# Modulation weights of a two-block network as fp32 products or as rounded halves and rests

## The reference, cut to what matters

```python
mod_x = (silu(c) @ w_mod + b_mod)[:, None, :]      # c: 1 x 1024, w_mod: 1024 x 6144
mod_c = silu(c_ctx) @ w_mod + b_mod
sh1, sc1, gt1, sh2, sc2, gt2 = split(mod_x, 6)     # and the same six of mod_c
h_x = rms_norm(x, g_norm1) * (1.0 + sc1) + sh1     # 256 x 1024
h_c = rms_norm(ctx, g_norm1) * (1.0 + csc1) + csh1
# h_x, h_c @ w_in: keys, values, gates ... ; later  x = x + gt1 * y_x,  and gt2, sc2, sh2
```

## Time and profile before

| | |
|---|---|
| median of 3 runs | 3134.74 us (3132.2 to 3134.81) |
| the profiled execution's own time | 3132.64 us |
| its span (first to last instruction) | 3130.8 us |
| mean granted TensorE clock | 0.956 |
| busy: PE, PEld, DVE, ACT, POOL | 92%, 76%, 63%, 49%, 6% |
| HBM read | 609.49 MB, 195 GB/s over the span |

### The profile page before, as it was taken

How to read it: one execution, slowest core, us unless ns; L and a number is a source line. 1 busy time by engine, 2 the same in 40 slices (tenths; PEclk the granted TensorE clock), 3 DMA queues, 4 the chain that set the end, 5 groups by cost and what they waited for, 6 DMA issues and landing times.

```text
span 3130.8 us, 42461 instructions
## 1 busy us (share of the span) xinstructions
PE 2866.4 (92%) x15757; PEld 2364.4 (76%) x15757; DVE 1960.3 (63%) x2198; ACT 1548.7 (49%) x1544; POOL 181.7 (6%) x204
## 2 busy tenths in 40 slices
PE   7999996999999998979999999999999999998997
PEld 1476785667666676758888897789788988977996
DVE  1345665888888888885568436554545674365554
ACT  2144444776777777663445444433334444354342
POOL 0000000000000000000036000000000440000000
PEclk9999997999999999998999999999989989999999
DMA  8522534898888989973243005544533430054454
GB/s 299 188 81 81 188 135 191 333 366 345 338 350 336 353 332 360 349 298 139 108 162 135 1 1 201 195 149 165 192 122 135 143 126 1 10 225 163 175 186 171
DMA packets 58072, 612.62 MB, mean 196 GB/s; under 512 B 12649, under 2 KB 18337, under 8 KB 21570
## 3 DMA queue, kind: packets, MB, share of 16 engines
q1 hardware_dynamic: 57922, 610.56, 51.6%
HBM read 609.49 MB, written 1.05 MB: 195 GB/s over the span
## 4 chain that ended last, share of the span: by engine, by line
issue 47%; PE 27%; DVE 10%; DMA 7%; POOL 5%; ACT 4%; DVEq 0%; SPq 0%; POOLq 0%; ACTq 0%
DVE arena_rounded L1514 7%; DMA weight_slabs<-in_expert_slabs 6%; ACT arena_rounded L1511 3%; PE psum_vector L562 3%; PE psum_vector L1567 2%; PE psum_vector L515 2%; PE psum_vector L517 2%; PE psum_vector L516 2%; POOL arena L3110 2%; PE psum_scalar L515 2%; PE psum_scalar L516 2%; PE psum_scalar L517 2%; PE psum_vector L1524 2%; PE psum_scalar L1554 2%; POOL arena L3113 2%
## 5 line engine op out<-in xcount | busy, mean ns | idle before, releaser
L1931 DVE TENSOR_TENSOR weight_slabs_rounded<-weight_slabs,arena_rounded 128x2048 fp32r<-128x2048 f32 x208 | 479.1, 2310 | 420.7 <-ACT arena_rounded L1928 403.4
L1514 DVE TENSOR_TENSOR arena_rounded<-weight_slabs,arena_rounded 128x2048 fp32r<-128x2048 f32 x290 | 651.9, 2287 | 62.9 <-ACT arena_rounded L1511 53.5
L1928 ACT ACTIVATE arena_rounded<-weight_slabs 128x2048 fp32r<-128x2048 f32 x208 | 396.2, 1913 | 455.6 <-PE psum_vector L517 261.4
L1511 ACT ACTIVATE arena_rounded<-weight_slabs 128x2048 fp32r<-128x2048 f32 x290 | 548.0, 1912 | 125.8 <-DMA weight_slabs<-in_expert_slabs 62.8
L515 PE MATMUL psum_vector<-arena_rounded,arena_rounded 128*128 128x512 f32 (+3 forms) x1312 | 480.1, 366 | 43.4 <-DVE weight_slabs_rounded L1931 30.8
L515 PE MATMUL psum_scalar<-arena_rounded,arena_rounded 128*128 128x256 f32 (+1 forms) x1456 | 476.2, 327 | 36.1 <-DVE weight_slabs_rounded L1931 15.5
L1554 PE MATMUL psum_scalar<-arena_rounded,arena_rounded 128*128 128x512 f32 x768 | 325.3, 424 | 71.8 <-DVE arena_rounded L1514 66.6
L517 PE MATMUL psum_vector<-arena_rounded,arena_rounded 128*128 128x512 f32 (+3 forms) x960 | 376.3, 392 | 0.0
L516 PE MATMUL psum_vector<-weight_slabs_rounded,arena_rounded 128*128 128x512 f32 x880 | 348.2, 396 | 0.0
L515 PEld LDWEIGHTS psum_scalar<-arena_rounded,arena_rounded 128*128 128x128 f32 x1456 | 283.4, 195 | 68.3 <-issue 13.5
L515 PEld LDWEIGHTS psum_vector<-arena_rounded,arena_rounded 128*128 128x128 f32 (+1 forms) x1312 | 257.6, 196 | 86.0 <-DVE weight_slabs_rounded L1931 41.2
(11 more groups left out here) (453 smaller groups left out, 4222.2 us busy)
## 6 DMA issues: line engine op xcount, KB each, us to landing
weight_slabs<-in_expert_slabs SPq DMA_DIRECT2D x145, 2048.0 KB, 9.1
weight_slabs<-in_layer_slabs SPq DMA_DIRECT2D x103, 2048.0 KB, 7.8
weight_slabs<-in_mixer_slabs SPq DMA_DIRECT2D x32, 2048.0 KB, 7.4
weight_slabs<-in_layer_slabs SPq DMA_DIRECT2D x6, 1024.0 KB, 5.4
arena<-in_mem SPq DMA_DIRECT2D x3, 1024.0 KB, 10.3
arena<-in_b_gate SPq DMA_DIRECT2D x6, 512.0 KB, 4.5
constants<-in_constants SPq DMA_DIRECT2D x1, 1025.0 KB, 5.0
arena<-in_x SPq DMA_DIRECT2D x1, 1024.0 KB, 7.2
```

Source lines behind the costliest of these rows:

```text
L1511: e.activation(high_, whole, ACT.Copy).then_inc(S("expert_high"), 1)
L1514: e.tensor_tensor(low, whole, high_.bitcast(F32), ALU.subtract).then_inc(S("expert_split"), 1)
L1928: e.activation(fr(high), low, ACT.Copy).then_inc(S("weights_high"), 1)
L1931: e.tensor_tensor(fr(low), low, fr(high).bitcast(F32), ALU.subtract).then_inc(S("weights_split"), 1)
```

## The change

Four rows take the place of two. ACT rounds silu(c) and silu(c_ctx) to a head each, DVE makes the rests; `c_parts` holds head and rest of c, head and rest of c_ctx. For slabs 1, 2, 4, 5, 6, 8, 9 and 10 the weights too are split, and a slab is 8 products with the head and 8 with the rest of the weights, all in rounded numbers, four stationary columns each. Slabs 0, 3, 7 and 11 stay fp32 products, of `c_whole` (the two vectors and two rows of zeros). The pairs of rows are added where rows become columns: the 16 transposes turn into 16 fp32 products of the 4-row result with a 4x2 table of ones and zeros; the gate rows add two rows in the same way. The heads of the mod slabs take turns at 64, 72, 88 and 96 KB. DVE and ACT split slab n + 1 before they turn to row n. The small loads move from behind slab 4 to behind slab 8, and ACT's order behind the evacuations changes with them.

```diff
-        for n in range(MOD_SLABS, len(MIX_SLABS)):
+        MIX_WHOLE = (0, 3, 7, 11)
+        MIX_SPLIT = [n for n in range(len(MIX_SLABS)) if n not in MIX_WHOLE]
+        MIX_RINGS = {1: (64, 72, 88, 96), 12: (88, 96, 104), 16: (112, 120, 128), 18: (120, 128), 20: (88, 128, 48), 26: (88, 120, 104)}
+        for n in MIX_SPLIT:
...
+        def mod_ahead(n):
+            return 2 * len([k for k in MIX_SPLIT if k <= min(n + 1, MOD_SLABS - 1)]) - 1
...
-                if n == 4:
+                if n == 8:
                     sp.wait_ge(S("set_by_pool"), 1)
...
+            def mod_rows(n):
                 w = slab()
                 bank = V.open()
+                if n in MIX_WHOLE:
+                    for k in range(KC):
+                        mm = pe.matmul(bank[0:4, :], c_whole[:, :, k], w[:, k, :], start=k == 0, stop=k == KC - 1)
+                    V.close(mm)
+                else:
+                    for i in range(2):
+                        high, low = half()
+                        for k in range(4):
+                            pe.matmul(bank[0:4, :], c_parts[:, :, 4 * i + k], high[:, k], start=i + k == 0, stop=False)
+                            mm = pe.matmul(bank[0:4, :], c_parts[:, :, 4 * i + k], low[:, k], start=False, stop=i == 1 and k == 3)
+                        if i == 0:
+                            used_now(mm)
+                    V.close(mm)
+                    used_by(V)
                 used(V)
...
-                    mm = pe.transpose(bank[:, 2 * j:2 * j + 2], modr[0:2, (first + j) * P:(first + j + 1) * P],
-                                      ident[0:2, 0:2])
+                    mm = pe.matmul(bank[:, 2 * j:2 * j + 2], modr[0:4, (first + j) * P:(first + j + 1) * P],
+                                   const("pair")[0:4, :], start=True, stop=True)
...
-                    V.close(pe.matmul(bank, ones[0:1, :], modr[0:1, at:at + BANK], start=True, stop=True))
+                    V.close(pe.matmul(bank, ones[0:2, :], modr[0:2, at:at + BANK], start=True, stop=True))
...
@@ ACT
-            e.activation(c2s, c2, ACT.Silu).then_inc(S("silu_c"), 1)
+            step(e.activation(c2s, c2, ACT.Silu))
+            e.activation(c_parts[:, 0:4:2, :], c2s, ACT.Copy).then_inc(S("silu_c"), 1)
...
+                weights.upto(mod_ahead(i))
+            weights.upto(mod_ahead(4))
             e.wait_ge(S("gain1_ready"), 1)
...
+                if k % 4 == 3:
+                    weights.upto(mod_ahead(5) - 1 + k // 4)
...
+            step(e.activation(hx[0], hx_whole, ACT.Copy))
+            weights.upto(mod_ahead(7))
+            step(e.activation(hc[0], hc_whole, ACT.Copy))
+            e.sem_inc(S("h_high"), 1)
+            for n in range(8, 10):
+                weights.upto(mod_ahead(n))
             e.wait_ge(S("small_weights_in"), 96)
...
@@ DVE
+            step.go(e.memset(c_whole, 0.0))
+            e.wait_ge(S("silu_c"), 1)
+            step.go(tt(c_parts[:, 1:4:2, :], c2s, c_parts[:, 0:4:2, :].bitcast(F32), ALU.subtract))
+            step.sync()
+            step(e.tensor_copy(c_whole[:, 0:4:2, :], c2s))
...
             def mod_rows(n):
-                V.give(e.tensor_copy(modr[0:2, n * BANK:(n + 1) * BANK], V.take()[0:2, :]), wait=True)
+                weights.upto(mod_ahead(n))
+                V.give(e.tensor_copy(modr[0:4, n * BANK:(n + 1) * BANK], V.take()[0:4, :]), wait=True)
...
-            for n in range(4, 11):
+            for n in range(4, 9):
                 mod_rows(n)
             e.wait_ge(S("h_high"), 1)
             step.go(tt(hx[1], hx_whole, hx[0].bitcast(F32), ALU.subtract))
+            mod_rows(9)
             step.go(tt(hc[1], hc_whole, hc[0].bitcast(F32), ALU.subtract))
+            mod_rows(10)
+            e.wait_ge(S("h_high"), 2)
```

More of the change, by code:

```diff
@@ L111 @@
                   ("solve", P * len(SOLVE)), ("thr", 1), ("eval", 1), ("bval", P), ("cg", GRP),
-                  ("c16", NE), ("freq", 24), ("half", 10), ("fold", SLOTS)):
+                  ("c16", NE), ("pair", 2), ("freq", 24), ("half", 10), ("fold", SLOTS)):
     CONST[_name] = (_at, _n)
@@ L147, in constant_table @@
     put("c16", np.repeat(16.0 - np.arange(NE)[None, :], P, 0))
+    put("pair", (np.arange(4)[:, None] // 2 == np.arange(2)[None, :]) * 1.0)
     fr = []
@@ L344, in build @@
         c2, c2s = tiny(2, KC), tiny(2, KC)
+        c_parts, c_whole = fr(room(81, 4, KC)), room(82, 4, KC)
         vec = tiny(24)
@@ L416, in mix_half @@
         def mix_half(g):
-            low = slabs[:, (MOD_SLABS + g // 2) % 3, 4 * (g % 2):4 * (g % 2) + 4, :]
+            low = slabs[:, MIX_SPLIT[g // 2] % 3, 4 * (g % 2):4 * (g % 2) + 4, :]
             return low, room(MIX_HIGH_AT[g], 4, BANK)
@@ L556, in pe_mixer @@
             V.close(pe.transpose(b[:, 0:88], vrow[0:88, :], ident[0:88, 0:88]))
[L558 to L569, removed]
-                    mm = pe.transpose(bank[:, 2 * j:2 * j + 2], modr[0:2, (first + j) * P:(first + j + 1) * P],
-                                      ident[0:2, 0:2])
[L572 to L594, removed]
-                    V.close(pe.matmul(bank, ones[0:1, :], modr[0:1, at:at + BANK], start=True, stop=True))
[L597 to L601, removed]
-                                  part_of(h, slice(None), k), start=k == 0, stop=k == KC - 1)
-            V.close(mm)
             n_half, n_used = 0, 0
@@ new lines, in mod_columns @@
+            def mod_columns(first):
+                pe.wait_ge(S("mod_rows"), first // 4 + 4)
+                bank = V.open()
+                for j in range(16):
+                    mm = pe.matmul(bank[:, 2 * j:2 * j + 2], modr[0:4, (first + j) * P:(first + j + 1) * P],
+                                   const("pair")[0:4, :], start=True, stop=True)
+                V.close(mm)
+            pe.wait_ge(S("silu_c"), 2)
+            for n in range(4):
+                mod_rows(n)
+            mod_columns(0)
@@ new lines, in pe_mixer @@
+            for n in range(4, 6):
+                mod_rows(n)
+            pe.wait_ge(S("xn_ready"), 1)
+            for k in range(KC):
+                bank = A.open()
+                for j in range(2 * NT):
+                    mm = pe.transpose(bank[:, j * P:(j + 1) * P], xn[:, j, k * P:(k + 1) * P], ident)
+                A.close(mm)
+            for n in range(6, MOD_SLABS):
+                mod_rows(n)
+            mod_columns(24)
+            pe.wait_ge(S("mod_rows"), 12)
+            for gt in (2, 5):
+                for side in range(2):
+                    at = gt * D + side * BANK
+                    bank = V.open()
+                    V.close(pe.matmul(bank, ones[0:2, :], modr[0:2, at:at + BANK], start=True, stop=True))
@@ L625, in half_product @@
+            pe.wait_ge(S("h_ready"), 1)
+            bank = V.open()
+            for i, h in enumerate((hx, hc)):
+                for k in range(KC):
+                    mm = product3(pe, bank[0:32, i * T:(i + 1) * T], part_of((fr(wlr_high), fr(wlr)), slice(None), k),
+                                  part_of(h, slice(None), k), start=k == 0, stop=k == KC - 1)
+            V.close(mm)
             def half_product(bank, h, w, i, t):
```

26 lines of the change are left out of this document (14 added, 12 removed).

## The result

The changed kernel takes 3146.28 us (median of 8 executions, 3139.61 to 3151.11), the kernel before, in the same batch, 3134.77 (8 executions, 3127.59 to 3138.51). The ratio is 1.0039, with 1.0025 to 1.0052 as its 95% interval: 11.5 us slower, 8 to 16 by the interval. The forecast was 7.1 us slower. The profiled execution has a span of 3143.4 us against 3130.8.

What follows compares the result with a forecast made beforehand. The first stage is bound by fp32 products on TensorE. Split slabs gain 6.0 us, columns take 2.5 back (3.5 gained), the clock costs 10.6: +7.1 us, 3139.7 against the profiled execution, 3141.8 against the median; range 3130 to 3148.

Steps and rivals of the forecast that it cites:

- its own case: Whole kernel: the clock falls and the change costs from +3.5 to +11 us; chance 0.57.
- The bound and the gain of split slabs: First stage, bound by fp32 products: split slabs make products 26 us cheaper, but gain only 6.0 at constant clock.
- Row 3: Ahead of the first columns: row 3 is copied behind slab 4's subtractions, at 48.1 us, so TensorE stands 3.1 us.
- Columns: Both column groups: pair-table products take 3.6 us instead of 1.15, 2.5 more twice, the second on the path.
- second rival: Both column groups: a price near 1.15 us gives 3126.2 us (chance 0.12), or 3133 with one clock fall (0.09).
- The clock in the stage: First stage: stalls and small products bring clock 0.50, costing 6.0 us kept at slab 5 and 3.0 later.
- The first rival: First stage: the clock holds through the stalls, 3.5 us gained, 3131.2 us; chance 0.14.
- The other reading of the transposes of x and ctx: Skill page: transposes don't count as busy, so slab 6 and slab 7's head run at half clock; sum +8.6 us.
- The clock in the tail: End of the stage: longer columns give low clock to all eight gate passes and the columns, 0 to 3.5 us.
- Small loads: Six loads moved behind slab 8: cost nothing; left behind slab 4, some 4 us of slab 5's lead.
- Third rival: Split slabs: rounded four-column products stream no faster than fp32 passes (0.43 us), 3145 to 3150 us; chance 0.08.
- Behind the stage: Everything after the first stage: shifted and not changed; more than 2 us of change means a cause outside the argument.

Runs made afterwards that it cites:

- x_whole: The changed kernel with all twelve slabs as fp32 products, none split: 3152.31 us, ratio 1.0047 to the kernel before.
- x_row3: The changed kernel with row 3 copied before slab 4's subtractions: 3138.84 us, ratio 1.0016 to the kernel before.
- x_transposed: The changed kernel with 16 four-row transposes per column group instead of pair-table products, DVE adding the pairs: 3136.15 us, ratio 1.0003 to the kernel before.
- after_again: The changed kernel, unaltered, profiled once more (the "second execution"): span 3138.9 us, slab 11's row copied at 114.55, low rank product at 133.99.
- y_whole6: The changed kernel with slabs 0, 3, 6 and 10 whole instead of 0, 3, 7 and 11: 3133.25 us, ratio 0.9988 to the kernel before.
- x_filled: The changed kernel with three unused fp32 products filling TensorE's wait for row 3: 3145.05 us, ratio 1.0020 to the kernel before.
- x_small4: The changed kernel with the small loads back behind slab 4: 3141.56 us, ratio 1.0018 to the kernel before.
- y_all: The changed kernel with slabs 0, 3, 6, 10 whole, columns as transposes, and row 3 copied first: 3124.76 us, ratio 0.9964 to the kernel before.
- x_both: The changed kernel with columns as transposes and row 3 copied before slab 4's subtractions: 3135.92 us, ratio 1.0004 to the kernel before.
- x_both_again: The x_both kernel, unaltered, profiled once more: span 3135.9 us against 3128.5 in its first profile.

## Why the prediction was right, and where it was off

The direction held, and the total was low by 4.4 us (7.1 against 11.5), just above the +11 at which the forecast ended its own case. Of the 4.4, 0.2 too much was put on the way to row 11, 1.8 too little on the tail behind it, and 2.8 lie behind the stage, where the forecast put nothing. All that it named as signs of being right came: the spacing of the split slabs' products, the wait for row 3, 32 records, the falls in both stretches and row 11 within 110 to 117.

- **The bound and the gain of split slabs.** Right. The products of split slabs are 0.22 apart, and the stage gains a small part of 26 us, since it then hangs on loads, halves and rests. Slab 5 was to end at 59.3 at constant clock and 6.0 later by the clock: 65.3; it ended at 64.75, and at 66.91 in the second execution. Slab 11's row was to come 3.0 later than before (-6.0 + 9.0) and came 2.8 later, 1.9 in the second pair. That it is so near is partly luck: the second execution got there by a later slab 5 and a shorter second half. The split into those two terms was only argued for slab 11: no run held the clock constant. x_whole bears out its size from the other side, with 4.2 us gained by splitting at the clock as it was.
- **Row 3.** Right: 3.26 of waiting against 3.1 (4.55 in the second execution), and the row copy done at 48.85 (48.18 + 0.67) against 48.1.
- **Columns.** Right. 32 records, 3.73 us at full clock (x_row3) against 3.6; the second rival (a price near 1.15) fell with it, and x_transposed is that rival made true: 9.7 us less at the low rank copy, and the slowdown gone from the median. For short columns with the clock falling in spite of them that rival had 2 us faster; measured is 0.6 slower.
- **The clock in the stage.** Right: 0.52 and 0.55 in 49 to 60, and again 0.66 in 80 to 85 and 0.55 in 100 to 105. The first rival (the clock holds) fell. The reason given, seven microseconds with almost nothing streaming, joins two things that the runs take apart in part. The stall alone was enough in after_again and x_transposed, where the clock fell before the columns began. The columns came with a fall in x_whole, with 0.83 of waiting ahead of them, and without one in x_row3, with the same 0.83. What decides between these two stays open. The other reading of the transposes of x and ctx, by which they would bring the clock down themselves and the sum would be +8.6, is nearer to the total and still not borne out: in y_whole6 all 32 lie in 62.98 to 69, no stall above 0.30 among them, and the clock is at 1.00 from 60 to 100.
- **The clock in the tail.** This is the mis-sized term. From row 11 to the low rank copy it was 13.5 us before and 19.4 after, 5.9 more; less the 2.5 of the columns, 3.4 is the clock's, out of 0 to 3.5. The text took 1.6; the upper end was right. By the windows 118 to 131 is all at 0.50 now. What was too small is the share of the gate passes and the low rank products that run at the low clock. This term too has two values: with the same products in the tail it took 19.4 in after, after_again, x_filled, 19.5 in x_row3 and y_whole6, but 16.3 in x_small4 and 16.6 in x_whole. In these two all 32 records of the second columns start 0.11 apart; in after, x_row3, x_filled and y_whole6 the last seven to ten are 0.21 apart. Where the fall comes later, less of the tail lies in it; what sets the moment stays open.
- **Small loads.** "Nothing" is not refuted: no run shows a gain from moving them, or a certain loss.
- **Third rival** (four columns stream no faster): refuted by 0.22 at 60 us.
- **Behind the stage.** Forecast: shifted and not changed, with a change of more than 2 us named as a sign of a cause outside the argument. The low rank copies, both executions of each kernel averaged, are 8.3 apart ((134.39 + 133.99 - 125.68 - 126.19) / 2), and the medians 11.5, with 8.3 still inside the interval. No steady extra shows in the traces. In the profiled pair the same VectorE copy, which is 8.7 later at the low rank product, is only 2.5 later at 1500 us (L2789 at 1498.95, in the kernel after L2828 at 1501.49), and the spans differ by 12.6: the distance shrinks and grows on the way; in the second pair the rest behind the stage differs by 0.5 (3004.9, 3004.4). Span less low rank copy went from 2999.4 (y_all) to 3017.6 (x_whole) over the thirteen profiles of this program's tail. So 3 us there lie within what executions differ by. But a median of 8 executions is steadier than one, so they stay open; whether a shifted start makes falls of the clock more frequent in later stages was not tested.

The Trainium skill, TensorE: Matmul & The Clock Gate, section LDWEIGHTS, was weighed in the forecast for the columns, 0.107 a load; the products with the pair table agree at full clock (0.11 from start to start in x_row3). The transposes of the earlier trace rows do not: they too load 128 columns each, and 16 loads take 1.06 us, less than 0.07 each.

```profile
112.04 1.06 PEld L570 LDWEIGHTS psum_vector<-constants,arena 2*128 2x128 f32 x16 [0.86 <-issue]
```

## What to carry to other kernels

When an operation is made cheaper on the bound engine, follow the others slab by slab: here 26 us of cheaper products became 4.2 in the stage (x_whole against the kernel after), as each split slab needs two copies, two subtractions and its load in a ring that turns no faster. Choose which pieces keep the old form by where the bound engine would otherwise wait: two whole slabs moved by one place were worth 15 us (from 11.5 slower than before to 3.8 faster). And price small products (few rows, few columns) with the clock that they leave behind: 32 instead of 16 in two groups cost 11 us (11.5 slower against 0.6), of which only 5 are their own length at full clock. A single profile can be several us from the median in the very stage that is studied; where the two disagree, profile again before a theory is built on it. And instructions ahead of an edit are a free check: if their times moved too, that part is not the edit's.

## What the runs showed of the hardware

- The clock falls or holds behind nearly the same stall from one execution to the next: 3.30 us of waiting left it at 1.00 in x_both and 3.63 brought 0.85 in x_both_again (80 to 103 us), but 3.30 and 3.31 brought 0.83 in x_small4 and after_again (100 to 110).
- Records of TensorE that keep it busy do not keep its clock: it was busy all of 118 to 131 in the kernel after and stood at 0.50, with gate rows of two partitions until 126.4 and rounded 256-column products, 0.21 apart, behind them; these were 0.11 apart only from 131.3 on.
- The same instructions met a different clock by execution: of the eleven microseconds from 49 to 60, 10.3 were at 0.50 in after, 11.0 in after_again and 6.8 in y_whole6, whose program is the same up to there. Filling the stall with 2.84 us of 512-column products (x_filled, 6.8) did not prevent the fall.
- At full clock a small fp32 product with the pair table is two records 0.11 apart (x_row3), and a transpose of 2 or 4 rows is one record, 0.06 from the next (before, x_both, y_all).
